# Tokens' scale moved behind the first projections, first units in another pass order, dummy products during the load of x, no permutation products, one address residue for the weights

## The reference, cut to what matters

```python
h = rmsnorm(x, g_mix_pre)              # x * rsqrt(mean(x^2) + eps) * g
proj = h @ w_in                        # q, k: 1024 columns, v: 512, u: 512
q = apply_partial_rope(q, cos, sin)    # first 16 of 64 dimensions of each head half turn
k = apply_partial_rope(k, cos, sin)
da = diff_attention(q, k, v, lam)
pooled = causal_multiscale_pool(u)
mix = concatenate([rmsnorm(da, g_subln) * (1 - lam_init), pool_mix(pooled)]) @ w_out
x = x + rmsnorm(mix, g_mix_post)
...
# second layer, retention branch: q and k of 4 heads x 128, all 128 dimensions turn
x1, x2 = x[..., :64], x[..., 64:]
rotary = concatenate([x1 * cos - x2 * sin, x1 * sin + x2 * cos])
```

## Time and profile before

| what | value |
|---|---|
| median of 3 runs | 1110.28 us (1110.19 to 1110.34) |
| the profiled execution's own time | 1110.75 us |
| its span | 1108.9 us |
| TensorE busy | 1073.8 us (97%) |
| VectorE busy | 708.4 us (64%) |
| ScalarE busy | 503.5 us (45%) |
| GpSimd busy | 31.2 us (3%) |
| HBM read | 181.61 MB, mean 165 GB/s |

### The profile page before, as it was taken

The page is one execution under the profiler, slowest core; times in us unless marked ns, Lnnn a source line. Parts: engine busy times, 40 slices in busy tenths (PEclk is TensorE's granted clock), DMA queues, the critical chain, the costliest instruction groups (busy, mean ns, idle before and its releaser), DMA issues.

```text
span 1108.9 us, 16809 instructions
## 1 busy us (share of the span) xinstructions
PE 1073.8 (97%) x6832; PEld 953.2 (86%) x6832; DVE 708.4 (64%) x897; ACT 503.5 (45%) x627; POOL 31.2 (3%) x47
## 2 busy tenths in 40 slices
PE   6999999999999999999999999999999999999997
PEld 6999898788888879989788888888999878888886
DVE  5768575368676445597667776446477667777642
ACT  5646465354444335655444444335522246443431
POOL 0100010000000001000000000000000000000000
PEclk9999999999999999999999999999999999999999
DMA  8833544245555546433145455554543144545521
GB/s 319 331 114 115 190 171 153 76 171 190 189 189 191 190 152 250 152 118 117 56 167 199 181 197 182 195 189 169 188 138 114 54 152 152 208 173 197 193 101 38
DMA packets 26714, 183.51 MB, mean 165 GB/s; under 512 B 3008, under 2 KB 3152, under 8 KB 5408
## 3 DMA queue, kind: packets, MB, share of 16 engines
q1 hardware_dynamic: 24912, 175.47, 44.3%
q0 software_dynamic: 1744, 7.20, 1.8%
HBM read 181.61 MB, written 1.05 MB: 165 GB/s over the span
## 4 chain that ended last, share of the span: by engine, by line
PE 89%; DVE 6%; ACT 2%; issue 1%; POOL 1%; DMA 1%; POOLq 0%; SPq 0%; DVEq 0%
PE GT L1569 12%; PE D L1569 10%; PE GT L1530 9%; PE GT L1532 9%; PE GT L1531 9%; PE D L1532 7%; PE D L1530 7%; PE D L1531 7%; PE GT L1572 5%; PE D L1572 4%; PE D L2081 2%; PE D L1625 1%; DVE s_wlo L859 1%; PE GT L1568 1%; POOL s_rstd L372 1%
## 5 line engine op out<-in xcount | busy, mean ns | idle before, releaser
L859 DVE TENSOR_TENSOR s_wlo<-s_raw,s_whi 128x2048 fp32r<-128x2048 f32 (+1 forms) x165 | 374.9, 2277 | 249.9 <-ACT s_whi L444 249.7
L444 ACT ACTIVATE s_whi<-s_raw 128x2048 fp32r<-128x2048 f32 (+1 forms) x165 | 312.8, 1904 | 161.2 <-PE D L1532 96.9
L1569 PE MATMUL GT<-s_x,s_whi 128*128 128x512 f32 x576 | 199.0, 394 | 1.8 <-DVE s_x L888 1.8
L1569 PE MATMUL D<-s_x,s_whi 128*128 128x512 f32 x480 | 165.6, 393 | 0.0
L1572 PE MATMUL GT<-s_x,s_wlo 128*128 128x256 f32 x504 | 141.8, 281 | 0.0
L1569 PEld LDWEIGHTS GT<-s_x,s_whi 128*128 128x128 f32 x576 | 104.5, 188 | 20.6 <-issue 2.3
L1572 PE MATMUL D<-s_x,s_wlo 128*128 128x256 f32 x420 | 118.1, 281 | 0.0
L1530 PE MATMUL GT<-s_x,s_whi 128*128 128x256 f32 (+1 forms) x392 | 112.1, 286 | 1.2 <-DVE s_x L888 1.2
L1532 PE MATMUL GT<-s_x,s_wlo 128*128 128x256 f32 (+1 forms) x392 | 109.8, 280 | 0.0
L1531 PE MATMUL GT<-s_x,s_whi 128*128 128x256 f32 (+1 forms) x392 | 109.4, 279 | 0.0
L1530 PE MATMUL GT<-s_whi,s_x 128*128 128x256 f32 (+1 forms) x344 | 106.9, 311 | 2.1 <-DVE s_x L1464 1.1
(11 more groups left out here) (322 smaller groups left out, 1644.2 us busy)
## 6 DMA issues: line engine op xcount, KB each, us to landing
s_raw<-in_stream SPq DMA_DIRECT2D x165, 1024.0 KB, 4.8
s_gb<-in_rows POOLq DMA_DIRECT2D x4, 512.0 KB, 4.2
s_xn<-in_x SPq DMA_DIRECT2D x2, 512.0 KB, 4.0
s_y<-in_mem POOLq DMA_DIRECT2D x1, 1024.0 KB, 11.3
s_w<-in_cmpw POOLq DMA_DIRECT2D x1, 1024.0 KB, 8.1
out<-s_y SPq DMA_DIRECT2D x4, 256.0 KB, 2.0
s_poolm<-in_poolm POOLq DMA_DIRECT2D x1, 768.0 KB, 14.6
s_retd<-in_retm POOLq DMA_DIRECT2D x1, 768.0 KB, 5.3
```

The lines of the kernel that those rows point to most:

```text
L444: nc.scalar.activation(whi[:, u % RING, 0:n], raw[:, u % RING, 0:n], ACT.Copy)\
L859: nc.vector.tensor_tensor(wlo[:, u % RING, 0:n], raw[:, u % RING, 0:n], whi[:, u % RING, 0:n], ALU.subtract).then_inc(lo_ready, 1)
L1569: ins = nc.tensor.matmul(o[:, f, :], hi[:, kt, c], x2[:, kt, :], start=kt == 0, stop=kt == KT - 1)
```

## The change

- **Tokens' scale.** x is transposed unscaled (`raw_transposes`: 16 transposes with the identity) and no longer waits for the means and the power. The gain of each feature is still put on by `norm_hi` and `norm_lo`. The token's scale is applied later: for v and u in `evac_scaled` (two ACT copies of 256 columns, one for each token tile, where one of 512 stood), for q and k through the tables: TensorE broadcasts `rstd` over the partitions (two float32 products of 128 columns behind unit 1), and VectorE multiplies both tables by it.
- **First units.** Unit 0's weights come as four transfers of 512 columns, and norm_hi, norm_lo and both splits of unit 0 go through them in four steps; `first_unit` multiplies in that order. `second_unit` makes all products with `whi` first and those with `wlo` last.
- **Queues.** The first constants and the gains are loaded from ACT's queue, the lambda vectors and the positions from POOL's; `gb` is loaded behind `poolm` and `wpool`.
- **Dummy products.** VectorE clears a part of `gb`, and TensorE multiplies it: two float32 products of 512 columns and one of 256.
- **No permutation products.** All eight `rotate` are gone. `rope_raw` now copies groups of partitions crosswise (4 copies of 32 partitions in the first layer, 2 of 64 in the second), the columns of w_in for q and k are reordered to suit, and the sine tables carry the sign.
- **One residue.** The pad ahead of `wlo` is gone and that ahead of `x2` is 32 floats: `wlo` now starts at the same address as `whi` modulo 128 bytes, and `x2` stays where it was. The constants are 256 floats shorter.

```diff
-        sb(ctx, "wlo_pad", [P, 16])
         wlo = sb(ctx, "wlo", [P, RING, UNIT], F32R)
-        sb(ctx, "x2_pad", [P, 16])
+        sb(ctx, "x2_pad", [P, 32])
...
-            sp.dma_start(cst[:, 0:CONST_FIRST], consts_in[:, 0:CONST_FIRST]).then_inc(sem("cst_first_in"), 16)
-            for j in range(RING):
+            for i in range(4):
+                sp.dma_start(raw[:, 0, 512 * i:512 * i + 512], stream[0, :, 512 * i:512 * i + 512])\
+                    .then_inc(sem(f"first_in{i}"), 16)
+            for j in range(1, RING):
...
+                w = 32 if which == "_a" else 64
+                for dst in range(0, P, w):
+                    ins = nc.scalar.activation(buf[dst:dst + w, j % 2, :], G[bank(u)][dst ^ w:(dst ^ w) + w, :],
+                                               ACT.Copy)
+                ins.then_inc(sem("rope_raw" + which), 1)
...
+            act.dma_start(cst[:, 0:CONST_FIRST], consts_in[:, 0:CONST_FIRST]).then_inc(sem("cst_first_in"), 16)
+            act.dma_start(gains[:, 0:GAIN["lam"][0]], gains_in[:, 0:GAIN["lam"][0]]).then_inc(sem("gains_in"), 16)
             norm_squares(0, xn, lambda c: chunk(y, c), parts=range(2))
-            split(0)
             act.wait_ge(sem("gains_in"), 16)
-            norm_hi(0, xTh)
+            for i in range(4):
+                norm_hi(0, xTh, (2 * i, 2 * i + 1))
+                act.wait_ge(sem(f"first_in{i}"), 16)
+                nc.scalar.activation(whi[:, 0, 512 * i:512 * i + 512], raw[:, 0, 512 * i:512 * i + 512],
+                                     ACT.Copy).then_inc(sem("first_hi") if i < 3 else hi_ready, 1)
...
+            def evac_scaled(u, dst):
+                act.wait_ge(unit_done, u + 1)
+                act.wait_ge(rstd_ready, pow_at("x0.1") + 1)
+                for t in range(NT):
+                    ins = nc.scalar.activation(dst[:, t, :], halves(G[bank(u)][:])[:, t, :], ACT.Copy,
+                                               scale=rstd[:, POW_COL[f"x0.{t}"]])
+                ins.then_inc(bank_read[bank(u)], 1)
...
+            dve.wait_ge(sem("rstd_wide"), 1)
+            for table in (cosT, sinT):
+                nc.vector.tensor_tensor(table[:], TB[1][:, 0:S], table[:], ALU.mult)\
+                    .then_inc(sem("tables_scaled"), 1)
...
+                for i in range(5):
+                    if i < 4:
+                        pe.wait_ge(sem("norm_hi"), 2 * i + 2)
...
+                        for kt in (2 * i, 2 * i + 1):
+                            for t in range(NT):
+                                step(t, kt, xTh, hi, start=kt == t == 0)
+                    if i >= 1:
+                        pe.wait_ge(sem("xT_ready"), 2 * i)
...
+                        for kt in (2 * i - 2, 2 * i - 1):
+                            for t in range(NT):
+                                step(t, kt, xTl, hi)
+                                ins = step(t, kt, xTh, lo, stop=kt == KT - 1 and t == 1)
...
-            norm_transposes(0)
+            pe.wait_ge(sem("warm_in"), 1)
+            for _ in range(2):
+                nc.tensor.matmul(TB[0][:], gb[:, 0:P], gb[:, 0:512], start=True, stop=True)
+            nc.tensor.matmul(TB[0][:, 0:256], gb[:, 0:P], gb[:, 0:256], start=True, stop=True)
+            raw_transposes()
             u0 = BASE["in"]
-            unit(u0, rows, ready=(sem("xT_ready"), 0))
-            unit(u0 + 1, rows)
+            first_unit()
+            second_unit(u0 + 1)
+            pe.wait_ge(rstd_ready, pow_at("x0.1") + 1)
+            for t in range(NT):
+                ins = nc.tensor.matmul(TB[1][:, P * t:P * t + P], rstd[:, POW_COL[f"x0.{t}"]].broadcast_to([P, P]),
+                                       ident, start=True, stop=True)
+            ins.then_inc(sem("rstd_wide"), 1)
...
-            rotate(0, "rot64", qraw, "_a")
             norm_transposes(1, y)
             unit(u0 + 6, columns)
-            rotate(1, "rot64", qraw, "_a")
+            pe.wait_ge(sem("tables_scaled"), 2)
...
-            rotate(0, "rot128", braw, "_b")
...
-                    if h < 3:
-                        rotate(1 + h, "rot128", braw, "_b")
                     if h < 6:
-                        if h < 4:
-
-                            pe.wait_ge(sem("rope_done_b"), h + 1)
                         unit(u0 + 8 + h, columns if h < 2 else rows)
```

More of the change, by code:

```diff
@@ L483, in rope_raw @@
                     act.wait_ge(sem("rope_done" + which), j - 1)
-                nc.scalar.activation(buf[:, j % 2, :], G[bank(u)][:], ACT.Copy)\
-                    .then_inc(sem("rope_raw" + which), 1)
+                w = 32 if which == "_a" else 64
[3 more added lines that the diff above has]
+                ins.then_inc(sem("rope_raw" + which), 1)
             def post_squares(k0, ph, n):
@@ L881, in norm_diag, with norm_lo @@
                     .then_inc(sem("diag_ready"), 1)
-            def norm_lo(n, dst_h, dst_l):
-                for kt in range(KT):
+            def norm_lo(n, dst_h, dst_l, kts=range(KT)):
+                for kt in kts:
                     if kt % 2 == 0:
@@ L1011, in _ @@
             norm_mean(0, "x0", 1)
-            dve.wait_ge(sem("cst_first_in"), 16)
-            norm_diag("x0", 0)
-            norm_diag("x0", 1)
-            split(0)
             dve.wait_ge(sem("gains_in"), 16)
-            norm_lo(0, xTh, xTl)
+            for i in range(4):
+                norm_lo(0, xTh, xTl, (2 * i, 2 * i + 1))
+                if i < 3:
+                    dve.wait_ge(sem("first_hi"), i + 1)
+                else:
+                    dve.wait_ge(hi_ready, 1)
+                c = slice(512 * i, 512 * i + 512)
+                nc.vector.tensor_tensor(wlo[:, 0, c], raw[:, 0, c], whi[:, 0, c], ALU.subtract)\
+                    .then_inc(sem("first_lo") if i < 3 else lo_ready, 1)
             split(1)
@@ L1611, in keep_clock, with raw_transposes @@
                 for _ in range(times):
-                    nc.tensor.matmul(bank_[:], ident, cst[:, 0:512], start=True, stop=True)
+                    nc.tensor.matmul(bank_[:], ident, same_rows(cst[:, 0:256], 2), start=True, stop=True)
+            def raw_transposes():
+                pe.wait_ge(sem("cst_first_in"), 16)
+                for t in range(NT):
+                    pe.wait_ge(sem(f"x_in{t}"), 16)
+                    for kt in range(KT):
+                        c = S * (kt % 2) + P * t
+                        ins = nc.tensor.transpose(DB[kt // 2][:, c:c + P], xn[:, t, P * kt:P * kt + P], ident)
+                        if t == NT - 1 and kt % 2:
+                            ins.then_inc(sem("norm_tr"), 1)
@@ new lines, in first_unit, with step @@
+            def first_unit():
+                hi, lo = (w[:, 0, :].rearrange("p (k n) -> p k n", k=KT) for w in (whi, wlo))
+                def step(t, kt, stat, mov, start=False, stop=False):
+                    return nc.tensor.matmul(G[0][:, 256 * t:256 * t + 256], stat[:, kt, P * t:P * t + P],
+                                            mov[:, kt, :], start=start, stop=stop)
+                for i in range(5):
+                    if i < 4:
+                        pe.wait_ge(sem("norm_hi"), 2 * i + 2)
+                        if i < 3:
+                            pe.wait_ge(sem("first_hi"), i + 1)
+                        else:
+                            pe.wait_ge(hi_ready, 1)
+                        for kt in (2 * i, 2 * i + 1):
[3 more added lines that the diff above has]
+                        pe.wait_ge(sem("xT_ready"), 2 * i)
+                        if i < 4:
+                            pe.wait_ge(sem("first_lo"), i)
+                        else:
+                            pe.wait_ge(lo_ready, 1)
+                        for kt in (2 * i - 2, 2 * i - 1):
+                            for t in range(NT):
+                                step(t, kt, xTl, hi)
+                                ins = step(t, kt, xTh, lo, stop=kt == KT - 1 and t == 1)
+                ins.then_inc(unit_done, 1)
@@ new lines, in second_unit @@
+            def second_unit(u):
+                hi, lo = (w[:, u % RING, :].rearrange("p (k n) -> p k n", k=KT) for w in (whi, wlo))
+                o = G[bank(u)]
+                pe.wait_ge(hi_ready, u + 1)
+                for t in range(NT):
+                    for kt in range(KT):
+                        c = slice(P * t, P * t + P)
+                        nc.tensor.matmul(o[:, 256 * t:256 * t + 256], xTh[:, kt, c], hi[:, kt, :],
+                                         start=kt == t == 0, stop=False)
+                        nc.tensor.matmul(o[:, 256 * t:256 * t + 256], xTl[:, kt, c], hi[:, kt, :], start=False,
+                                         stop=False)
+                wait_unit(u)
+                for t in range(NT):
+                    for kt in range(KT):
+                        ins = nc.tensor.matmul(o[:, 256 * t:256 * t + 256], xTh[:, kt, P * t:P * t + P], lo[:, kt, :],
```

(3 more changed lines are left out.)

59 lines of the change are left out of this document (22 added, 37 removed).

## The result

| | before | after |
|---|---|---|
| median (range), us | 1110.34 (1110.19 to 1111.34) | 1104.48 (1102.73 to 1105.69) |
| profiled execution, us | 1110.75 | 1102.73 |
| its span, us | 1108.9 | 1100.9 |

The ratio is 0.9942, 95% interval 0.9930 to 0.9955. The prediction was 1101.7, with 1096 to 1106.5 as its range: faster, within the range, 2.8 us above the number. The profiled execution is the quickest of the five: it shows the mechanism, and the distance from it to the median has to be explained apart.

The account below looks back on a forecast made before the run. TensorE, busy 97% of the span, was taken as the bound. First layer 5.5, second layer's rotations 3.1 and residue 0 sum to 8.6 us, giving a median of 1101.7 us, range 1096 to 1106.5.

Parts of the forecast that it names:

- first layer: Earlier start and removed rotations, up to the end of the first layer's start: 5.5 us saved, bounds 3.5 and 7.5.
- second layer's rotations: Four permutation products removed from TensorE in the second layer: 3.1 us saved, bounds 1.5 and 4.0.
- residue: Start address of wlo modulo 128 bytes, affecting TensorE's product groups: taken as 0, between -7 and +13 us.
- so `split(1)` on ScalarE ends at 15.5: Start: unit 1 lands at 13.6 us, so ScalarE's split of it ends at 15.5; VectorE got it at 18.97 before.
- VectorE's chain moves only from 18.97 to 15.5: Start: VectorE's work to the cosine's end stays 17.7 us, so the cosine ends at 33.2 and unit 4 starts 4.7 early.
- the start is given back: Rival: split(1) comes late, VectorE's chain starts at 18, first layer keeps 1.0 to 1.5 us: 1106.2; chance 0.13.
- The crosswise copies: ScalarE's rope_raw: 32 partitions taken to cost what a full copy does, so a set grows from 0.6 to 2.4 us.
- Third and fourth rotation: First layer: removing the third keeps 0.8 us, kv unit 5.5 early; the fourth is lost to TensorE's wait for the probabilities.
- a drift through the MLPs: Sign in the profile: if the lead drifts through the MLPs instead of staying constant, the residue acts and zero is wrong.
- The rival that it hurts: Rival: wlo at whi's residue collides in the MLPs, 10 ns x 1320 groups = 13.2 us: 1114.9; chance 0.07.
- the first unit runs cold: Rival: clock at 1.2 GHz in unit 0, its 48 products take about 4.3 us more, 0.8 hidden: 1105.2; chance 0.14.

Follow-up runs that it names:

- run 6: Changed kernel with the second layer's permutation products, whole copies and waits for the turned block put back: 1107.24 us, ratio 0.9970.
- run 5: Kernel before with only the two new pads (none ahead of wlo, 32 columns ahead of x2): 1109.52 us against 1110.61, ratio 0.9993.
- run 8: Changed kernel with the first layer's crosswise copies made one whole copy each, leaving out the exchange of rotated rows: 1102.87 us, ratio 0.9931.
- run 4: Changed kernel with the two old pads (16 floats ahead of wlo, 16 ahead of x2): 1104.77 us, ratio 0.9939.
- run 1: The changed kernel again, unaltered, for its spread: 1105.14 us, ratio 0.9943.
- run 3: Changed kernel without the three dummy products and the clear: 1104.10 us, ratio 0.9941.
- Run 12: Changed kernel with sines behind the third unit's bank, memory's parts ahead of the splits, and two more dummy products behind x's transposes: 1101.05 us, ratio 0.9914.
- run 9: Changed kernel with sines behind the third unit's bank and the first crosswise copy ahead of the wait for mem and its squares: 1105.81 us, ratio 0.9963.

## Why the prediction was right, and where it was not

**The sum, term by term**, against the profiled executions (8.02 us apart; 8.6 forecast):

| term | forecast | measured | by |
|---|---|---|---|
| first layer | 5.5 (3.5 to 7.5) | 3.7 | lead from 93 to 222 us |
| second layer's rotations | 3.1 (1.5 to 4.0) | 3.1 | run 6 |
| residue | 0 (-7 to +13) | 1.1 gained | run 5, profiled |
| together | 8.6 | 7.9 | |

The sum came out within 0.7 us partly by luck: the first layer gave 1.8 us less than forecast, and the residue, taken as nothing, gave 1.1. That the three measured terms are the right ones is borne out on the way, for run 5's lead over the kernel before is 0.4, 1.5, 0.6 and 1.1 us at 415, 753, 918 us and the end. Added to 3.7, and behind the second layer's rotations to 3.1 more, that gives 4.1, 8.3, 7.4 and 7.9, where the leads of after are 4.1, 8.3, 7.5 and 8.0.

**The start: the step that failed** is "so `split(1)` on ScalarE ends at 15.5" and "VectorE's chain moves only from 18.97 to 15.5". I let unit 1 land 2.5 us behind unit 0's last byte and took no more landings into the sum. Unit 1 was split from 14.35 and unit 2 only from 17.22, so the chain began at 16.30 and had a gap of 0.58; the cosine ended at 34.67 and not at 33.2. The mechanism held: TensorE waits at unit 4 for `evac_scaled`, behind the sines, and the wait is 2.00 us where I had 0.8. Unit 4 is 3.1 us early (4.7 forecast), and from there everything is late by the same 1.5: mem lands at 41.2 (39.9), the low parts end at 57.98 (56.7), the pooling starts 3.1 us early (4.7). I had worked out the wait of 1.18 there as 1.4. The rival "the start is given back" thus came true in part. Its price was too high by the prediction's own steps: a chain that starts 2.5 us later takes 2.5 us from the 5.5, not 4.0 to 4.5.

**The crosswise copies** took 2.39 us a set, the 2.4 that I took from the earlier trace rows: 32 partitions cost what 128 cost (0.60, run 8). Run 8 shows that they are on the path, for the 1.18 us of the wait at the pooling.

**Third and fourth rotation.** The third was kept: the lead at the scores is 4.6 with the fourth's 0.86 in it, so 3.7 at the end of the `kv` unit. The fourth was lost, as forecast: the wait of 0.95 comes up at 82.5 us and the lead goes back to 3.73.

**The second layer** came out by its own steps: L2066 starts a lead of 4.07 behind a wait of 1.42 (1.5 forecast), where the lead had been 4.80 behind the first removed product, and the three others with the bank's wait are kept.

**The residue.** "The value I take is 0" was wrong by 1.1 us, and the sign that the text gives for it, a drift through the MLPs, is what the leads show: 3.7 to 4.1 across the first, 7.9 to 8.3 across the second. The rule of the Trainium skill (SBUF — State Buffer, Who interferes with whom) that I had set beside it, that TensorE's two read ports are its own, would have the residue change nothing; moving the start of `wlo` by 64 bytes changed a group of three products by 16 ns (runs 4 and 5). The measurement decides. The rival that it hurts priced all groups alike at 10 ns; the groups go both ways, and nearly cancel.

**The rest of the miss: the median is not the profiled run.** I carried the 0.47 us between median and profile of the kernel before over to the kernel after. After has a median 1.75 us above its profiled run, the other way round. 1101.7 + 0.6 (the sum) + 0.45 (the offset) + 1.75 = 1104.5. The 1.75 is put down to dips of the clock: run 1 shows two of them for 1.27 and 1.5 us, and the mean clocks of the ten runs fit; the median run itself has no trace. The rival "the first unit runs cold" named the right cause and the wrong place. Where the first unit was slow (run 3 as a whole, runs 4 and 6 from about 12 us on), the wait for the bank of unit 2 shrank from 2.00 us to nothing or 0.16 and the loss at 58 us was 0.5 us at most; in runs 4 and 6 there was none. The prediction had said that: what is lost in the first units is covered by this wait. What costs is a dip behind it.

**Open.** What brings a dip about is not shown. In 11 traces with the dummies, the first unit has a dip in six. Leaving out the two with extra products, the pause ahead of the first unit was 2.49, 2.63, 3.27, 3.31 and 3.31 us in the five with the dip, and 1.52, 1.66, 1.82 and 2.09 in the four without. But something else separates all eleven: the moment at which the clock first rose, which each trace shows as the halving of the distance between products (the transposes' falls from 0.21 to 0.11 us). It rose at 4.95 to 5.91 us in the six with the dip and at 6.03 to 7.58 in the five without. An early rise also ends the transposes sooner and so lengthens the pause, which makes the two hard to tell apart. Run 12 tells them apart once: its pause was only 1.30 us, its clock rose at 5.31, and it has the dip. Why the rise moves between executions no run shows. The dips near 37 us (runs 1 and 8) stand behind waits of 1.92 and 2.01 us, but the kernel after had 2.00 and none; the one near 61 us (run 9) stands behind 3.03. The ones near 464 us (runs 1 and 4) have no wait ahead of them, only products of 15 columns, which stand there in every trace. No run took the place near 464 by itself.

## What to carry to other kernels

A wait that ends last on TensorE is worth removing together with the next one in its chain (2.0 us removed alone gave 0.4 in the trace, all of it from an earlier landing, both together 3.1), and work that is due later, here the weight splits, goes behind what the next product waits for. Where landings pace the start, every landing of the stretch belongs in the sum, not the first alone. Predict the profiled run and the median apart, and before two traces are compared, look at the clock of both and then follow the starts of the same instructions.

## What the runs showed of the hardware

- TensorE's granted clock fell to 1.2 GHz for a short stretch in the midst of unbroken products, in 8 of the 12 traces of the changed kernel and its variants, at one or two places each, and in neither of the traces of the kernel before and of it with the new pads; one such stretch cost 1.5 to 1.6 us where nothing covered it (run 1 near 464 us, run 9 near 61 us).
- With the same dummy products from 1.47 us on, the clock rose to 2.4 GHz at 4.95 to 7.58 us in eleven traces, so not at a fixed time.
- A copy on ScalarE of 512 columns out of PSUM takes 0.60 us for 32 partitions (2.39 / 4), for 64 and for 128 (run 8).
- The residue of a weight buffer's address moved TensorE's groups of three in the down projection by 16 ns of 696 (quicker with `wlo` at `whi`'s residue), and the wide units' pairs the other way, by some 2.4 ns of 353 (runs 4 and 5).
- The clock's column reads 1.00 ahead of its first record: the count of products in the window tells the level there.
